# Expert layer with the weight blocks as the stationary operand, two parts of the tokens moving side by side

## The reference

```
def moe_swiglu(x, router, w_gate, w_up, w_down):
    logits = (x @ router).astype(f32)
    top_v, top_i = lax.top_k(logits, TOP_K)            # TOP_K = 2 of N_EXPERTS = 8
    top_w = jax.nn.softmax(top_v, axis=-1)
    combine = jnp.sum(jax.nn.one_hot(top_i, N_EXPERTS) * top_w[..., None], axis=-2)
    for e in range(N_EXPERTS):
        out = out + combine[..., e:e+1] * (silu(x @ w_gate[e]) * (x @ w_up[e])) @ w_down[e]
```

## Time and profile before

| | us |
|---|---|
| median of 3 runs (range) | 1938.23 (1937.34 to 1939.71) |
| profiled execution, its own time | 1937.1 |
| its span, first to last instruction | 1935.3 |
| busy PE / PEld / DVE / ACT in the span | 1859.4 / 1572.3 / 1545.1 / 1193.3 |
| expert stage, first matmul to start of the last | 937.21 to 1914.56 |

### The profile page before, as it was taken

One profiled execution on the slowest core, in us unless ns is written; L12 is line 12 of the kernel. 1 busy time (PEld: TensorE's weight loads), 2 busy tenths in 40 slices (PEclk: granted clock), 3 DMA queues, 4 the chain that ended last, 5 costly groups with the idle time before them and its releaser, 6 DMA issues.

```text
span 1935.3 us, 31827 instructions
## 1 busy us (share of the span) xinstructions
PE 1859.4 (96%) x11947; PEld 1572.3 (81%) x11947; DVE 1545.1 (80%) x1758; ACT 1193.3 (62%) x1274; POOL 345.1 (18%) x441
## 2 busy tenths in 40 slices
PE   8789989999999999999999999999999999999995
PEld 8788989999999988898677777777777777777774
DVE  6988886657647868865788888888888888888886
ACT  4236646544444366454767777677677776767775
POOL 7974100079800041000000000000000000000000
PEclk9899999999999999999999999999999999999998
DMA  5447644455555556546699999999999999999996
GB/s 188 140 154 221 198 153 159 138 197 185 197 177 167 180 161 217 173 159 259 233 365 373 375 365 375 356 374 377 351 383 363 371 378 361 371 362 369 381 362 238
DMA packets 106564, 527.53 MB, mean 273 GB/s; under 512 B 21879, under 2 KB 23319, under 8 KB 62519
## 3 DMA queue, kind: packets, MB, share of 16 engines
q1 hardware_dynamic: 96727, 489.80, 68.8%
q0 software_dynamic: 8688, 35.35, 6.2%
q10 hardware_dynamic: 1056, 1.08, 0.2%
HBM read 505.69 MB, written 20.50 MB: 272 GB/s over the span
## 4 chain that ended last, share of the span: by engine, by line
PE 53%; DVE 5%; issue 3%; ACT 3%; DMA 1%; DVEq 0%; ACTq 0%; POOL 0%; POOLq 0%; SPq 0%
PE bank L675 16%; PE bank L677 16%; PE bank L676 16%; DVE s5m_parts L2052 2%; PE bank L1093 1%; ACT zone_parts L1454 1%; DVE ring_parts L1521 1%; DVE s5m L1541 1%; PE bank L714 0%; PE bank L1125 0%; DMA s5m<-in_experts 0%; DMA x_rows<-work 0%; PE bank L1035 0%; DVE zone L1652 0%; PE bank L913 0%
## 5 line engine op out<-in xcount | busy, mean ns | idle before, releaser
L2052 DVE TENSOR_TENSOR s5m_parts<-s5m,ring_parts 128x2048 fp32r<-128x2048 f32 x228 | 519.4, 2288 | 69.9 <-ACT ring_parts L1454 68.9
L1454 ACT ACTIVATE ring_parts<-s5m 128x2048 fp32r<-128x2048 f32 x228 | 431.4, 1918 | 74.7 <-DMA s5m<-in_experts 73.9
L1521 DVE TENSOR_TENSOR ring_parts<-ring,ring_parts 128x1024 fp32r<-128x1024 f32 x238 | 313.6, 1325 | 167.5 <-ACT ring_parts L1152 166.5
L675 PE MATMUL bank<-uT_parts,ring_parts 128*128 128x264 f32 x1312 | 383.3, 292 | 31.3 <-DVE ring_parts L1521 27.3
L676 PE MATMUL bank<-uT_hi,ring_parts 128*128 128x264 f32 x1312 | 376.8, 287 | 0.0
L677 PE MATMUL bank<-uT_hi,ring_parts 128*128 128x264 f32 x1312 | 376.1, 287 | 0.0
L1152 ACT ACTIVATE ring_parts<-ring 128x1024 fp32r<-128x1024 f32 x238 | 250.9, 1056 | 189.9 <-PE bank L677 151.8
L675 PE MATMUL bank<-s5m_parts,work_parts 128*112 128x512 f32 x896 | 358.4, 400 | 1.9 <-DVE s5m_parts L2052 1.9
L2052 DVE TENSOR_TENSOR s5m_parts<-s5m,zone_parts 128x2048 fp32r<-128x2048 f32 x112 | 255.8, 2289 | 53.6 <-ACT zone_parts L1454 53.4
L675 PEld LDWEIGHTS bank<-uT_parts,ring_parts 128*128 128x128 f32 x1312 | 252.0, 192 | 40.6 <-issue 35.3
L677 PE MATMUL bank<-ring_parts,work_parts 128*112 128x512 f32 x640 | 253.3, 396 | 0.0
(11 more groups left out here) (353 smaller groups left out, 3149.0 us busy)
## 6 DMA issues: line engine op xcount, KB each, us to landing
s5m<-in_experts SPq DMA_DIRECT2D x340, 1024.0 KB, 6.3
ring<-in_weights SPq DMA_DIRECT2D x238, 512.0 KB, 3.3
work<-in_sret POOLq DMA_DIRECT2D x8, 512.0 KB, 5.9
zone<-in_sret POOLq DMA_DIRECT2D x8, 512.0 KB, 4.3
out_ret_s<-work POOLq DMA_DIRECT2D x8, 512.0 KB, 5.9
s5m<-kscr POOLq DMA_DIRECT2D x2, 2048.0 KB, 15.5
out_ret_s<-zone POOLq DMA_DIRECT2D x8, 512.0 KB, 6.1
xT<-in_xT SPq DMA_DIRECT2D x1, 1056.0 KB, 5.4
```

The source lines that it names most:

```text
L675: pe.matmul(out, left[0], right[1], start=first, stop=False)
L1454: act.activation(high_slot(c), slot(c, s5m), ACT.Copy).then_inc(high_done, 1)
L1521: dve.tensor_tensor(weights(c, ring_parts), weights(c, ring), f32(weights_hi(c)), ALU.subtract).then_inc(low_done, 1)
L2052: dve.tensor_tensor(slot(c, s5m_parts), slot(c, s5m), f32(high_slot(c)), ALU.subtract).then_inc(low_done, 1)
```

## The change

The two operands change places. `_columns` lays the expert weights out in 128 by 128 blocks, 16 to a chunk, and each block is now the stationary side. For a block, `expert_chunk` issues two matmuls instead of a share of three: the high part of the block against the high and low part of the tokens side by side (2 x 104 moving columns), and the low part of the block against the high part of the tokens (104 columns). The output has the hidden unit on the partitions, so the four transposes of each hidden tile go. A bank holds for two hidden blocks (`GROUP`) the sum of high x high and low x high in its first half and high weight x low token in its second. ACT copies the second half to SBUF (`cross_out`) and TensorE adds it to the first by a product with the identity (`add_cross`). For down ACT and DVE add the two halves (`down_low_out`, `down_out`), and the result is turned to token rows by `rows_of`. `CAP` goes from 112 to 104. The first two chunks of an item are issued at the end of the item before (`TURNED`), also after the last item, where their result is not used.

```diff
-CAP = 112
+CAP = 104
+GROUP = 2
+E_GROUPS = F_EXP // GROUP
+GU = F_EXP
+TURNED = GROUP
...
+            def expert_chunk(item, ahead, c):
+
+                t, i = c // GROUP, c % GROUP
+                count = lambda per, n: per * ahead + n if item is None else item * per + per * ahead + n
+                if i == 0:
+                    for b in (gate_at(t), up_at(t)):
+                        pe.wait_ge(evicted[b], count(USES[b], BASE[b] + t // 3))
+                pe.wait_ge(low_done, count(E_CHUNKS, N_CHUNKS + c + 1))
+                for x in range(2 * KD):
+                    k = x % KD
+                    w = slice(x * P, (x + 1) * P)
+                    high, low = high_slot(c)[:, w], slot(c, s5m_parts)[:, w]
+                    out = halves(up_at(t) if x >= KD else gate_at(t))
+                    if k == KD - 1:
+                        pe.matmul(out[:, i, 0], low, xg[:, 0, k * CAP:(k + 1) * CAP], start=False, stop=False, skip_group_check=True)
+                    mm = pe.matmul(out[:, i], high, xg[:, :, k * CAP:(k + 1) * CAP], start=(k == 0 and i == 0), stop=(k == KD - 1),
+                                   skip_group_check=True)
+                    if k < KD - 1:
+                        mm = pe.matmul(out[:, i, 0], low, xg[:, 0, k * CAP:(k + 1) * CAP], start=False, stop=False, skip_group_check=True)
+                mm.then_inc(mm_done, 1)
+
+            def add_cross(t, count):
+
+                pe.wait_ge(cross_ready, count(t + 1))
+                for h, b in ((0, gate_at(t)), (1, up_at(t))):
+                    mm = pe.matmul(halves(b)[:, :, 0], ident_parts[:, :], cross_parts[:, t % 2, h].rearrange("p (f c) -> p f c", f=GROUP),
+                                   start=False, stop=True, skip_group_check=True)
+                mm.then_inc(cross_added, 1)
...
-                for t in range(E_TILES):
-                    expert_tile(t % 2, t, 4 * t)
-                    if t > 0:
-                        hidden_transpose(t - 1)
-                    expert_tile(2 + t % 2, t, 4 * t + 2)
...
+                for c in range(TURNED, GU):
+                    expert_chunk(it, 0, c)
+                    if c % GROUP == 0:
+                        add_cross(c // GROUP - 1, lambda n: it * E_GROUPS + n)
...
+                for b in GATHER_AT:
+                    bank_free(b, USES[b])
+                for c in range(TURNED):
+                    expert_chunk(it, 1, c)
+                bank_free(6, 2)
+                rows_of((KD - 2, KD - 1))
...
+            def down_low_out(tiles, b, done):
+
+                act.wait_ge(mm_done, done + MM_BASE)
+                act.activation(ysb[:, tiles, :], halves(b)[:, :, 1], ACT.Copy).then_inc(down_low, 1)
+
+            def cross_out(t, done):
+
+                act.wait_ge(mm_done, done)
+                for h, b in ((0, gate_at(t)), (1, up_at(t))):
+                    last = act.activation(cross_parts[:, t % 2, h].rearrange("p (f c) -> p f c", f=GROUP), halves(b)[:, :, 1], ACT.Copy)
+                last.then_inc(cross_ready, 1)
...
+def _columns(w):
+
+    k, m = w.shape
+    return w.reshape(k // P, P, m // P, P).transpose(2, 1, 0, 3).reshape(m // P, P, k)
```

More of the change, by code:

```diff
@@ L552, in vec, with gate_at, up_at, halves @@
             return vecs[:, c:c + 1]
[L556 to L563, removed]
-        MISC0 = 3
[L566 to L572, removed]
+        GATHER_AT, INDEX_AT, ROWS_AT = (1, 4), 0, (2, 7)
+        BASE = [sum(1 for i in set(PLACE.values()) if i % NBANK == b) + (b in GATHER_AT or b == INDEX_AT) for b in range(NBANK)]
+        USES = [5 + 1, 5 + 1, 4 + 1, 5, 5 + 1, 4 + 1, 2, 1 + 1]
+        M_INDEX, M_ROWS, M_Y = 1, 2, 4
+        MISC = 5
+        MISC0 = 3
+        def gate_at(t):
+            return t % 3
+        def up_at(t):
+            return 3 + t % 3
+        def halves(b):
+            return bank[b][:, 0:2 * GROUP * CAP].rearrange("p (f w c) -> p f w c", f=GROUP, w=2)
         TURNS = E_CHUNKS // MRING
@@ L1034, in gather @@
                         n = UT[i][1]
-                        mm = pe.matmul(bank[2 + 2 * half][0:CAP, :], sel_first[0:n, i, :],
+                        mm = pe.matmul(bank[(2, 5)[half]][0:CAP, :], sel_first[0:n, i, :],
                                        xtok[i][0:n, half * WIDE:(half + 1) * WIDE], start=(i == 0), stop=(i == 2))
@@ L1041, in gather @@
                         c = (4 * half + x) * P
-                        mm = pe.transpose(bank[1 + 2 * half][:, x * CAP:(x + 1) * CAP], ytok[0:CAP, c:c + P],
+                        mm = pe.transpose(bank[GATHER_AT[half]][:, x * CAP:(x + 1) * CAP], ytok[0:CAP, c:c + P],
                                           ident[0:CAP, 0:CAP])
@@ new lines, in add_cross, with rows_of @@
+            def add_cross(t, count):
[4 more added lines that the diff above has]
+                mm.then_inc(cross_added, 1)
+            def rows_of(tiles):
+                for d in tiles:
+                    mm = pe.transpose(bank[ROWS_AT[d // 4]][0:CAP, (d % 4) * P:(d % 4 + 1) * P], ysb[:, d, :], ident[:, :])
+                    if d in (3, KD - 1):
+                        mm.then_inc(misc_done, 1)
@@ L1444, in gathered @@
                     k = 4 * half + x
-                    last = act.activation(xg_hi[:, k, :], bank[1 + 2 * half][:, x * CAP:(x + 1) * CAP], ACT.Copy,
+                    last = act.activation(xg[:, 0, k * CAP:(k + 1) * CAP], bank[GATHER_AT[half]][:, x * CAP:(x + 1) * CAP], ACT.Copy,
                                           scale=vec(DEPTH - 1, V_GF, k))
@@ L1458, in _ @@
                 act.wait_ge(first_rows, half + 1)
-                act.activation(ytok[0:CAP, half * WIDE:(half + 1) * WIDE], bank[2 + 2 * half][0:CAP, :], ACT.Copy
+                act.activation(ytok[0:CAP, half * WIDE:(half + 1) * WIDE], bank[(2, 5)[half]][0:CAP, :], ACT.Copy
                                ).then_inc(first_out, 1)
@@ L1487, in _ @@
                     high_experts(it, c + AHEAD)
                 act.wait_ge(now_ready, it * 2 + 2)
[L1490 to L1492 removed]
+                for half, b in enumerate(ROWS_AT):
+                    act.wait_ge(misc_done, it * MISC + MISC0 + M_Y + half)
+                    act.activation(ytok[0:CAP, half * WIDE:(half + 1) * WIDE], bank[b][0:CAP, :], ACT.Copy,
+                                   scale=weight_now[0:CAP, :]).then_inc(evicted[b], 1)
```

228 lines of the change are left out of this document (130 added, 98 removed).

## The result

The changed kernel takes 3334.55 us (median of 4 runs, 3334.19 to 3343.26), the kernel before, run beside it, 1938.88. The ratio is 1.7211, with a 95% interval of 1.718 to 1.7241. Slower was forecast, but at 2214 us and at most 2310.

A forecast was written before the change was run, and what follows sets the result against it. TensorE's column streaming was taken to bound the expert stage, then its weight loads: 11,040 at 0.1117 us, 155.7 us an item, a stage of 1252.7 us instead of 977.4, 1 us at the end; 2214 us, range 2168 to 2310.

The forecast's parts named there:

- the sum: Expert stage: 8 items of 155.7 us plus 7.1 us of turned chunks, 1252.7 us instead of 977.4.
- the clock falls: Rival, expert stage: TensorE drops to the 1.2 GHz level, 0.218 us a load, about 3390 us in all; chance 0.03.
- rows 2: Profile window of one expert item before the change: 121.8 us, PE busy for 121.3, clock at 1.00 throughout.
- The rows of 20 loads at 0.50: Earlier trace, after the engine had waited: 20 loads took 4.34 us, 0.218 each, at a granted clock of 0.50.
- The price of a load: Expert stage: each load of 128 columns takes 0.1117 us, whether 208 or 104 columns stream behind; bounds 0.108 and 0.1206.
- Loads hide: Rival, expert stage: a block takes 153 ns, DMA bounds at 2.77 us a chunk, about 1896 us in all; chance 0.07.
- What cost nothing: Expert stage: DVE, ACT, DMA and the `cross_ready` wait stay hidden behind TensorE's 3.57 us a chunk.
- Banks come back three groups later: Expert stage: claim that banks are free again three groups later, listed among what costs nothing.

The follow-up runs named there:

- e_piece128: The kernel before, with each expert-stage matmul of 512 columns cut into four of 128, each with its own load; 3860.54 us.
- e_lift: The changed kernel, with the low block streaming both token parts (208 columns for 104) in chunks 2, 3 and 4 of each item alone; 2269.98 us, ratio 1.1709.
- e_grouped: The changed kernel, with the low-part product read as bf16 and a chunk's 16 low products placed behind its 16 high ones; 1981.95 us, ratio 1.0239.
- e_cap: The kernel before with `CAP` of 104 instead of 112 and nothing else; 1933.12 us, ratio 0.9977.
- e_high: The changed kernel with the product of the low part of the block left out; 1921.53 us.
- e_wide: The changed kernel, with the low block streaming both token parts (208 columns for 104) everywhere; 2263.22 us, ratio 1.1678.
- e_lift_stop4: The changed kernel with 208-column low products in chunks 2 to 4, next-item transposes and their gather wait moved ahead of down's chunk 4; 2584.14 us.
- e_piece256: The kernel before, with each matmul of 512 columns cut into two of 256, each with its own load; 1994.54 us.

## Why the prediction was wrong

**The step that failed** is the clock of the sum: all 11,040 loads were priced at 0.1117 us, the price at 1.00, and the rival "the clock falls" had a chance of 0.03 on this ground: "Against it: the window of rows 2 is at 1.00 throughout, and the engine will not stand still between loads." Its time, about 3390 us, was within 2% of the measured 3334.6. The ground was wrong twice. Between loads the engine doesn't stand still, but it does at the start of the stage and at the turn of the loop, which were not looked at. And that window shows the clock under streams of 512 columns; it says nothing on whether other work brings a fallen clock back. The rows of 20 loads at 0.50 after a stop showed the clock down between stops of 1.7 and 2.5 us, and I used them for a price only (0.218; with the 0.33 us that a record takes at 0.50 in place of 0.19 it is 0.211, against 0.213 measured).

**What took its place.** A standstill brings the clock to 0.50. There a load takes 0.213 us, and 208 and 104 columns behind two loads left it there for hundreds of microseconds; with 208 behind every load it came back within some 10 us. At 1.00 it stayed up with the same 208 and 104 for 157 us, an item's length. So the state kept itself.

How many columns stream behind a load isn't all that counts, though. In the kernel before, the clock came back behind the 20 loads of the earlier trace rows, which have only 128 columns each, 0.218 us apart; the window behind them, where the earlier trace rows had 0.50, is

```profile
927.60:934.00 6.40, 6.28 (x17) 1.97 (x15) 1.69 (x1) 1.21 (x3) 0.00 (x0) 1.00 0.00 1
```

while in e_piece128 `fp32r` matmuls of 128 columns stayed at 0.50 for 2716 us. Those 20 products, like the six transposes behind which the clock also rose, are of unrounded operands. Whether the kind of operand makes the difference, no run tested.

**The terms of the sum.** The price of a load was right: 0.112 against 0.1117, also where 104 columns stream behind. e_lift turns the forecast into a measurement: with the clock at 1.00 for nearly all of the stage, and 39 of 42 chunks as in the changed kernel, the time is 2270 us, inside the range of 2168 to 2310. The 56 us over 2214 are two terms that I left out: 7.7 us of stop at the start of the stage with some 8 more for 17 us of slow clock behind it, and some 6 us at each of the seven turns (161.6 between falls of the clock in e_lift against 155.7 for an item), of which 3.2 to 4.0 are the stop and the rest the slow clock behind it. The rest of the distance is the clock: the stretches at 0.50 in the stage sum to 2318 us (293.5 + 873.8 + 276.5 + 873.8), and work that is bound by loads would have taken 0.112 / 0.213 of that, 1099 us less; 3334.6 - 1099 = 2235, and with a stop and a slow stretch at the turns that would then be at 1.00 throughout, it is close to the 2270 of e_lift.

**Loads hide.** The rival of 0.07 is excluded for the `fp32r` operands that it spoke of (rows at 1.00 above); in runs of bf16 the load does hide (0.046 a pair in e_grouped). The Trainium skill ("TensorE: Matmul & The Clock Gate", section "Back-to-back issue gap") gives 81 ns for a pair of 128 columns; the `fp32r` pairs here take 112 with 104 columns and with 208, so the trace doesn't agree; bf16 pairs of 104 columns took 46, and none of 128 was run.

**What cost nothing** was forecast rightly but for one bank: at no place in the list of waits does PE wait for `cross_ready`, and DVE, ACT and DMA are all behind TensorE. "Banks come back three groups later" missed bank 0 at the start of the stage, which came back 7.5 us late. `CAP` gains 0.2% by itself.

**Open.** Why the stop at the turn is there. It came in all kernels with a long loop body (their instruction queue moves 146 to 210 packets) and in none with a short one (65 before and in e_cap, 67 in e_high). In e_wide a packet of that queue starts 0.6 to 1.0 us behind the last matmul at each of the seven turns, and the next 4.0 to 4.3 us behind it; in e_high six of the seven turns have none. So fetching instructions at the branch is likely, but no run changed that alone. The stop was 3.2 to 5.0 us where the clock was 1.00 ahead of it. At the four turns of the changed kernel that were reached at 0.50, a packet came 2.4 to 2.6 us before the last matmul ended, and the stop was 0.3 us at most. Nor is it settled why the clock rises behind the six transposes ahead of the turn in four of the eight items of the changed kernel and in all eight of e_lift_stop4, and how short a stop can be: most falls lay in or behind stops of 3.2 us or more, some behind less (1.6 us in e_grouped, 2.2 in e_high).

## What to carry to other kernels

Ask of each stage not only whether TensorE will be busy, but where it stands still for some microseconds (its start, the turn of a loop, a gather), and what runs right behind that stop: here 48 products an item of 208 columns in place of 104 brought the clock back and were worth 1065 us. And before 128-column blocks are put on the stationary side: a load of an `fp32r` block cost 112 ns at clock 1.00 with 104 columns behind it and with 208, so by an estimate from these rows fewer than some 245 columns (112 / 0.457) are paid as if there were that many.

## What the runs showed of the hardware

- The level of the clock depends on what came before: the same pairs ran for 157 us at 1.00 and for 873 us at 0.50. Each fall in the expert stage lay in or behind a stop of TensorE, of 3.2 us or more in most cases and of 1.6 and 2.2 us in a few (e_grouped, e_high); a stop of 7.3 us that was put in brought it down in both kernels.
- At 0.50 `fp32r` pairs of 208 and 104 columns left the clock down for up to 873 us; with 208 behind every load it was back within some 10 us; and 20 unrounded products of 128 columns brought it back in the kernel before.
- At 0.50 a load of 128 `fp32r` columns takes 0.213 us, 0.112 at 1.00.
- A bf16 load's record is 0.10 us. In turns with `fp32r` the two pairs took 0.22 us together; in runs of its own type a pair took 0.046 us.
- Kernels with some 1,050 matmuls and their loads (e_piece256) or more in the body of the loop had a stop of 3.2 to 5.0 us at its turn when they reached it at clock 1.00; with some 720 (e_high) it was 0.4 at most.
